# Output product of a hybrid block as four column groups of Strassen's seven products, in place of sixteen straight weight blocks

## The chip, the cores and the metric

The kernel runs on one core of a Trainium2 chip. Its time is device microseconds of one execution, median of several runs. A profiled execution of the same program gives the trace; its span and its own time stand in the table below.

## What is computed

One layer of a block with three branches (gated delta rule, S5 state space, cross attention with a memory) for 512 rows of 2048 channels in float32. The change touches only the end of it:

```
gates = sigmoid(gate_raw).reshape(b, s, 3, D)
merged = gates[:, :, 0] * p_a + gates[:, :, 1] * p_b + gates[:, :, 2] * p_c
h = h + merged @ w_out[l]          # [512 x 2048] @ [2048 x 2048]
return rmsnorm(h, final_g)
```

Every float32 product runs as three fp32r products: each operand is split in a rounded part and what the rounding left, and high x high, high x low and low x high are summed in PSUM.

## The kernel before

The program is written engine by engine, with an explicit semaphore for each hand-over; nothing reorders the instructions of an engine. TensorE is called PE below, VectorE DVE, ScalarE ACT, GpSimd POOL, SyncE SP. Constants: P = 128, S = 512, D = 2048, KW = 8 tiles of 1024, KD = 16 tiles of 2048, NT = 4 row tiles.

Weights come in blocks of 128x2048 floats, alternating between two slots. SP loads a block into `raw` in two halves, ACT copies each half to `wh` (L442, rounded), DVE writes `raw - wh` to `wl` (L450), and PE waits for that. A half is free again when PE has counted `w_used`.

Before the output product three branch products run (`products`, 8 blocks each). DVE multiplies each result by its gate from PSUM (L2261) and adds it to `merged` (L2263). In the third branch ACT and DVE also split each finished tile of `merged` into `uh` and `ul` (L1635, L2248). The moving operand is 512 columns wide.

The output product (`output`, called for four column groups `c` of 512 columns) takes 16 blocks B_OUT to B_OUT + 15. A block holds four k tiles; for each, and for each of four row tiles `m`, three matmuls of 128x512 add into bank 4 * (c % 2) + m. In all that is 4 x 16 x 4 x 3 = 768 matmuls. At a group's end DVE adds the residual `xr` from PSUM (L2297), ACT squares the sum (L1665) for the norm, DVE multiplies by the gain `fg` (L2313), and POOL only issues the next loads of `xr` (L778). In the last group the row tiles end one after another; for each, sum, root, reciprocal and scaling follow (L2302 to L2308, L1671), and SP stores two halves of the row tile.

POOL computes only in the mixer stage, from about 440 to 1490 us, where it makes tables and demodulates the S5 states (L663, L664, L666, tensor_tensor instructions of 128x512 with both inputs in SBUF) beside DVE's L450.

## Time and profile before

| | us |
|---|---|
| median of 3 runs | 2097.92 (2096.86 to 2097.95) |
| profiled execution, its own time | 2097.53 |
| its span | 2095.8 |
| PE busy | 2067.8 (99%) |
| DVE busy | 1267.3 (60%) |
| ACT busy | 804.7 (38%) |
| POOL busy | 744.7 (36%) |

The span is the profiled program from its first to its last instruction; the execution's own time is 1.7 us more. The profiled execution lies within 0.4 us of the median. PE's busy time counts a matmul from its start until its result is out, and consecutive ones overlap, so a stretch is measured by the starts of matmuls, not by their length. The starts of DVE and ACT instructions also overlap the ends of those before by about 0.1 us.

### The profile page before, as it was taken

Reading aid. Unit: us, or ns where it says so; the run is one execution under the profiler, and the core shown is the slowest. Engines: PE = TensorE matmul, PEld = TensorE weight load, DVE = VectorE, ACT = ScalarE, POOL = GpSimd, SP = SyncE. Lnnn points to the kernel's source line nnn. Section 1 sums busy time; section 2 is a strip of 40 time slices with the busy share of each in tenths; the row PEclk is TensorE's granted clock in tenths of the full one; section 3 lists DMA queues with packets and bytes.
Section 4 is the critical chain, followed back from the end, with each engine's and each line's share of the span. In section 5 each row is a group of like instructions: output and inputs, shape, how many; then the busy total and the mean of one; then the engine's idle time right before and its main releaser. Section 6 shows DMA issues by size and latency. Waiting matters only on the chain.

```text
span 2095.8 us, 30735 instructions
## 1 busy us (share of the span) xinstructions
PE 2067.8 (99%) x12124; PEld 1691.8 (81%) x12124; DVE 1267.3 (60%) x1779; ACT 804.7 (38%) x1055; POOL 744.7 (36%) x555
## 2 busy tenths in 40 slices
PE   7999999999999999999999999999999999999998
PEld 6799888888787787877878778777778888888886
DVE  6554353439688596885968959676433335454333
ACT  5433232353344533445334443453242222232223
POOL 0000000038576585765857658577201000100000
PEclk9999999999999999999999999999999999999999
DMA  8244343453343433434334343343356565553334
GB/s 258 61 127 135 102 134 91 114 135 91 104 116 94 121 97 104 115 95 120 97 104 114 96 117 100 104 117 102 103 169 207 173 184 150 180 151 110 112 123 149
DMA packets 382913, 260.63 MB, mean 124 GB/s; under 512 B 23769, under 2 KB 351810, under 8 KB 382146
## 3 DMA queue, kind: packets, MB, share of 16 engines
q1 hardware_dynamic: 364146, 203.16, 35.6%
q0 software_dynamic: 11408, 43.00, 5.9%
q10 hardware_dynamic: 7232, 12.72, 1.6%
q8 instruction: 87, 1.43, 0.3%
q14 instruction: 40, 0.33, 0.1%
HBM read 223.17 MB, written 27.28 MB: 119 GB/s over the span
## 4 chain that ended last, share of the span: by engine, by line
PE 94%; DVE 2%; DMA 1%; ACT 1%; issue 1%; POOLq 0%; ACTq 0%; DVEq 0%
PE bank L456 29%; PE bank L458 28%; PE bank L457 28%; PE bank L1097 1%; PE bank L979 1%; PE bank L991 1%; DMA yst<-s_out 1%; DVE wl L450 1%; PE bank L1046 0%; PE bank L1087 0%; PE bank L952 0%; PE bank L1035 0%; PE bank L1088 0%; PE bank L1077 0%; PE bank L1060 0%
## 5 line engine op out<-in xcount | busy, mean ns | idle before, releaser
L456 PE MATMUL bank<-uh,wh 128*128 128x512 f32 x2048 | 826.1, 403 | 2.9 <-DVE wl L450 2.7
L458 PE MATMUL bank<-uh,wl 128*128 128x512 f32 x2048 | 799.3, 390 | 0.0
L457 PE MATMUL bank<-ul,wh 128*128 128x512 f32 x2048 | 799.0, 390 | 0.0
L450 DVE TENSOR_TENSOR wl<-raw,wh 128x1024 fp32r<-128x1024 f32 x352 | 468.6, 1334 | 476.3 <-ACT wh L442 475.0
L442 ACT ACTIVATE wh<-raw 128x1024 fp32r<-128x1024 f32 x352 | 370.2, 1058 | 552.2 <-DMA raw<-in_w_in_dram 182.0
L456 PEld LDWEIGHTS bank<-uh,wh 128*128 128x128 f32 x2048 | 384.7, 188 | 90.5 <-issue 10.0
L458 PEld LDWEIGHTS bank<-uh,wl 128*128 128x128 f32 x2048 | 384.4, 188 | 83.5
L457 PEld LDWEIGHTS bank<-ul,wh 128*128 128x128 f32 x2048 | 385.2, 188 | 74.1 <-issue 1.9
L622 POOL DMA_DIRECT2D gated_c<-ox x8 | 4.3, 543 | 372.6 <-DVE ox L1808 371.9
L663 POOL TENSOR_TENSOR hr<-tcos,gr 128x512 f32<-128x512 f32 x32 | 51.7, 1615 | 199.4 <-DVE gi L2138 199.3
L1449 ACT ACTIVATE gk<-bank 128x512 f32<-128x512 f32 x48 | 28.7, 598 | 192.0 <-PE bank L458 192.0
L456 PE MATMUL bank<-gh,wh 128*128 128x512 f32 x256 | 100.9, 394 | 0.0
L458 PE MATMUL bank<-gh,wl 128*128 128x512 f32 x256 | 100.4, 392 | 0.0
L456 PE MATMUL bank<-wh,uh 128*128 128x512 f32 x256 | 99.6, 389 | 0.0
L458 PE MATMUL bank<-wh,ul 128*128 128x512 f32 x256 | 99.6, 389 | 0.0
L457 PE MATMUL bank<-wl,uh 128*128 128x512 f32 x256 | 99.6, 389 | 0.0
L457 PE MATMUL bank<-gl,wh 128*128 128x512 f32 x256 | 99.4, 388 | 0.0
L740 POOL DMA_DIRECT2D gates<-gates x24 | 17.1, 712 | 207.8 <-DVE merged L2263 136.1
L456 PE MATMUL bank<-mh,wh 128*128 128x256 f32 x256 | 73.6, 288 | 5.5 <-DVE wl L450 5.5
L458 PE MATMUL bank<-mh,wl 128*128 128x256 f32 x256 | 72.6, 283 | 0.0
L457 PE MATMUL bank<-ml,wh 128*128 128x256 f32 x256 | 72.5, 283 | 0.0
L664 POOL TENSOR_TENSOR karg<-tsin,gi 128x512 f32<-128x512 f32 x32 | 64.8, 2026 | 0.0
(355 smaller groups left out, 2826.1 us busy)
## 6 DMA issues: line engine op xcount, KB each, us to landing
raw<-in_w_in_dram SPq DMA_DIRECT2D x224, 512.0 KB, 3.9
raw<-in_w_kv_mem_dram SPq DMA_DIRECT2D x32, 512.0 KB, 4.0
raw<-in_w_out_dram SPq DMA_DIRECT2D x32, 512.0 KB, 3.6
gates<-gk ACTq DMA_DIRECT2D x48, 256.0 KB, 4.3
gates<-gates POOLq DMA_DIRECT2D x24, 512.0 KB, 4.7
raw<-in_s_w_glu_dram SPq DMA_DIRECT2D x16, 512.0 KB, 4.0
raw<-in_w_br_c_dram SPq DMA_DIRECT2D x16, 512.0 KB, 3.9
raw<-in_w_br_a_dram SPq DMA_DIRECT2D x16, 512.0 KB, 4.0
```

Source lines behind the costliest of these rows:

```text
L442: act.activation(k.wh[slot][:, c], k.raw[slot][:, c], ACT.Copy).then_inc(k.w_hi, 1)
L450: dve.tensor_tensor(k.wl[slot][:, c], k.raw[slot][:, c], k.wh[slot][:, c].bitcast(F32), ALU.subtract).then_inc(k.w_lo, 1)
L456: pe.matmul(o, ah, bh, start=start, stop=False)
L457: pe.matmul(o, ah, bl, start=False, stop=False)
L458: return pe.matmul(o, al, bh, start=False, stop=stop)
L663: pool.tensor_tensor(o[:, :], c1[:, :], a[:, :], ALU.mult).then_inc(k.dem, 1)
L664: pool.tensor_tensor(k.karg[:, :], c2[:, :], b[:, :], ALU.mult).then_inc(k.dem, 1)
L740: pool.dma_start([k.gates0, k.gates1][m % 2][:, :, :], k.gates_d[row:row + 2 * P, :] .rearrange("(t p) s -> p t s", p=P)).then_inc(k.gt_in ...
L979: mm = pe.matmul(ps[2][r:r + B, n * B:(n + 1) * B], k.lbt[r:r + B, n, :], k.tb[r:r + B, n, :], start=True, stop=True)
L991: mm = pe.matmul(ps[6][r:r + B, n * B:(n + 1) * B], k.ub[r:r + B, n, :], k.xb5[r:r + B, n, :], start=True, stop=True)
L1097: mm = pe.matmul(ps[5][r, :], k.bc[:, n, r], h[q][:, :], start=n == 0, stop=n == 1)
L1449: act.activation(k.gk[n][:, :], o[:, :], ACT.Sigmoid).then_inc(k.mx_out, 1)
```

## The change

The output product is rewritten as Strassen's scheme on halves. `merged` (transposed, channels on partitions) is cut into low and high channels (tiles i and KW + i) and into the first and last 256 rows; `w_out` into upper and lower rows and into left and right columns. Seven products of 256x1024x256 blocks replace eight. The columns are taken in four groups `g`; a group has eight units `t` (one k tile of each half), so there are 32 units `n`. A unit has seven products, each of 2 x 3 matmuls with 256 moving columns: 42 matmuls. Each product of a group has a PSUM bank of its own; the eighth bank lets the next group begin. In the last group products 2 and 3 are left to the end and summed straight in PSUM (`last_row`, 96 matmuls), so that a unit there has 30.

For each unit, SP loads four pieces of 128x256 of `w_out` to `wr` (three slots). Per unit the engines then do:

- POOL `weight_differences`: one subtraction of 128x256.
- ACT `copy_second` (128x256), `weights_x` (128x768, in the last group 128x256), `weights_y` (128x1024): the copies that round.
- DVE `weight_sums` (128x512), `weights_x` (128x768, in the last group 128x256), `weight_sums_two` (128x512), `weights_y` (128x1024). All of them have both inputs in SBUF.

Both engines, and POOL, wait with unit n + 1 until PE has finished unit n - 1 (`y_part`), since `wph` and `wpl` have two slots.

The sums of `merged` are made by POOL (`merged_sums`, four instructions of 128x256 for each of eight pairs, the last two pairs after the last merge), and are split by ACT and DVE as tiles of 128x768; the low tiles of `merged` are split only in the first units (`LATE`, `EARLY`, `SUMS` list which unit carries which: eight and two tiles of 128x512, two of 128x768). At a group's end ACT copies products 1, 2 and 3 out of PSUM, DVE combines products 6, 7, 4 and 5 with them (five instructions of 128x512, each with one input in PSUM), and POOL makes the six additions to `hrow` (`add_first`, `add_shared`) and four multiplications by the gain (`row_gains`), all of 128x2x256 with both inputs in SBUF, during the units t = 0 to 4 of the next group. `hrow` is preloaded with x. In the third branch the low and high parts of the activations now use `uh` and `ul` instead of `gh` and `gl`, and the branch tiles are taken in pairs that alternate between the low and the high half.

The core of the diff:

```diff
...
+            k.wr = sb(area, "wr", [3, 4, QC])
...
+            k.sxh = sb(area, "sxh", [3, KW, QC], F32R)
+            with ExitStack() as a:
+                k.sraw = sb(a, "sraw", [3, KW, QC])
+            k.sxl = sb(area, "sxl", [3, KW, QC], F32R)
...
+QC = 256
+GROUPS = D // (2 * QC)
+UNITS = GROUPS * KW
+ORDER = (1, 2, 3, 6, 7, 4, 5)
+FIRST = (3, 2, 6, 4, 5, 1, 7)
+SHARED = (1, 6, 7, 4, 5)
+PIECE = {1: 0, 3: 1, 2: 2, 5: 3, 7: 4, 6: 5, 4: 6}
+Y_PART = slice(3, 7)
+
...
+    def output_weights(n):
+
+        g, t = divmod(n, KW)
+        if n == 0:
+            sp.wait_ge(k.gb_st0, 8 * KW)
+            sp.wait_ge(k.gb_st1, 8 * KW)
+        if n < 3:
+            sp.wait_ge(k.w_hi, 2 * (B_OUT - 2) + n + 1)
+        wait(sp, k.w_sum, 2 * (n - 2))
+        if n > 2:
+            sp.wait_ge(k.m_sum, differences_done(n - 3))
+            sp.wait_ge(k.w_hi, rounded(n - 3, 0))
+        wait(sp, k.w_lo, x_part(n - 3) if n > 2 else 0)
+        for half in range(2):
+            row = (t + KW * half) * P
+            sp.dma_start(k.wr[:, n % 3, 2 * half:2 * half + 2, :],
+                         k.w_out[row:row + P, :].rearrange("p (h c) -> p h c", h=2)[:, :, g * QC:(g + 1) * QC]).then_inc(k.w_in_half[n % 3], 16)
+
+    def input_columns(g):
+
...
+    def last_weights(v):
+
+        n = UNITS + v
+        sp.wait_ge(k.w_sum, 2 * min(n - 2, UNITS))
+        sp.wait_ge(k.m_sum, differences_done(min(n - 3, UNITS - 1)))
+        sp.wait_ge(k.w_lo, x_part(n - 3) if n - 3 < UNITS else last_part(n - 3 - UNITS))
+        for t in (2 * v, 2 * v + 1):
+            row = (KW + t) * P
+            sp.dma_start(k.wr[:, n % 3, 2 * (t % 2):2 * (t % 2) + 2, :],
+                         k.w_out[row:row + P, :].rearrange("p (h c) -> p h c", h=2)[:, :, (GROUPS - 1) * QC:GROUPS * QC]).then_inc(k.w_in_half[n % 3], 16)
+
...
+    def merged_sums(i):
+
+        lo, hi, s = k.merged[:, i, :], k.merged[:, KW + i, :], k.sraw
+        n = sums_done(i) - 4
+        if i == 0:
+            pool.wait_ge(k.g_lo, 3 * KW)
+        tt = pool.tensor_tensor
+        tt(s[:, 0, i, :], lo[:, QC:S], hi[:, QC:S], ALU.add).then_inc(k.m_sum, 1)
+        pool.wait_ge(k.m_sum, n + 1)
+        tt(s[:, 1, i, :], s[:, 0, i, :], lo[:, 0:QC], ALU.subtract).then_inc(k.m_sum, 1)
+        tt(lo[:, QC:S], lo[:, 0:QC], lo[:, QC:S], ALU.subtract).then_inc(k.m_sum, 1)
+        pool.wait_ge(k.m_sum, n + 2)
+        tt(s[:, 2, i, :], hi[:, 0:QC], s[:, 1, i, :], ALU.subtract).then_inc(k.m_sum, 1)
...
+    def weight_differences(n):
+
+        w = k.wr[:, n % 3, :, :]
+        pool.wait_ge(k.w_in_half[n % 3], 8 * B_OUT + 32 * (n // 3 + 1))
+        if n < 2:
+            pool.wait_ge(k.w_used, 2 * (B_OUT - 1 + n))
+        else:
+            pool.wait_ge(k.w_used, y_part(n - 2))
+        pool.tensor_tensor(k.wyr[n % 2][:, 6, :], w[:, 2, :], w[:, 3, :], ALU.subtract).then_inc(k.m_sum, 1)
...
+    def row_gains(g, m):
+        pool.wait_ge(k.h_sq, 4 * g + TAIL_ROWS.index(m) + 1)
+        o = output_columns(k, [m], g)
+        pool.tensor_tensor(o, o, k.fg[:, :, :], ALU.mult).then_inc(k.h_fg, 1)
+
+    def add_first(g):
+
+        pool.wait_ge(k.xr_in, 64 * (g + 1))
+        for half, n, v in ((1, 1, k.gk0), (1, 2, k.c2), (0, 3, k.c3)):
+            if g == GROUPS - 1 and n > 1:
+                continue
+            pool.wait_ge(k.o_p1, 3 * g + n)
+            if n == 2:
+                pool.wait_ge(k.o_add, 6 * g + 1)
+            o = quarter(k, 0, half, g)
+            pool.tensor_tensor(o, o, halves(v[:, 0:S]), ALU.add).then_inc(k.o_add, 1)
+
+    def add_shared(g, part):
+
+        rows, half, v = ((1, 1, k.t3), (1, 0, k.t3), (0, 0, k.gk1))[part]
+        pool.wait_ge(k.o_ev, 5 * g + 3 + part)
+        if part == 2 and g < GROUPS - 1:
+            pool.wait_ge(k.o_add, 6 * g + 3)
+        o = quarter(k, rows, half, g)
+        pool.tensor_tensor(o, o, halves(v[:, 0:S]), ALU.add).then_inc(k.o_add, 1)
 
...
+    for n in range(3, UNITS):
+        g, t = divmod(n, KW)
+        if n + 1 < UNITS:
+            weight_differences(n + 1)
+        if t == 0 and g:
+            add_first(g - 1)
+        if t == 1 and g:
+            add_shared(g - 1, 0)
+            add_shared(g - 1, 1)
+        if t == 2 and g:
+            add_shared(g - 1, 2)
+            pool.wait_ge(k.fg_in, 16 * g)
+        if t in (3, 4) and g:
+            for m in (2, 3) if t == 3 else (0, 1):
+                row_gains(g - 1, m)
+        if t == 5 and g:
+            pool.wait_ge(k.h_fg, 4 * g)
+            load_gains(g)
+    add_first(GROUPS - 1)
+    for part in range(3):
+        add_shared(GROUPS - 1, part)
 
...
+    def product(n, p, last_x, last_y):
+
+        g, t = divmod(n, KW)
+        r = ORDER.index(p)
+        bank = ps[(7 * g + r) % 8]
+        if p in (1, 2, 3):
+            pe.wait_ge(k.w_lo, x_part(n))
+        else:
+            pe.wait_ge(k.w_lo, y_part(n))
+        if g == 0:
+            pe.wait_ge(k.m_lo, operand_count("low" if p in (1, 7) else "high" if p in (2, 4) else "sums", t))
+        if n == 0:
+            wait(pe, k.mrg, {4: 2 * KD - 2, 5: 2 * KD - 1}.get(p, 2 * KD - 3 if p == 7 else 0))
+        elif t == 0 and r == 0:
+            if g == 1:
+                pe.wait_ge(k.mrg, 2 * KD)
+            wait(pe, k.o_ev, 5 * (g - 1))
+        elif t == 0 and r < 4:
+            pe.wait_ge(k.o_p1, 3 * (g - 1) + r)
+        elif t == 0:
+            pe.wait_ge(k.o_ev, 5 * (g - 1) + r - 3)
+        order = product_order(n)
+        after_x = t == KW - 1 and p == order[order.index(last_x) + 1]
+        after_unit = t == 0 and r == 0 and g
+        hi, lo = operand(p, t)
+        wh, wl = k.wph[n % 2][:, PIECE[p], :], k.wpl[n % 2][:, PIECE[p], :]
+        for i in range(2):
+            a, o = slice(i * P, (i + 1) * P), bank[:, i * QC:(i + 1) * QC]
+            mm = pe.matmul(o, hi[:, a], wh, start=t == 0 and i == 0, stop=False)
+            if i == 0 and (after_x or after_unit):
+                mm.then_inc(k.w_used, 1)
+            pe.matmul(o, hi[:, a], wl, start=False, stop=False)
+            mm = pe.matmul(o, lo[:, a], wh, start=False, stop=t == KW - 1 and i == 1)
+        if t == KW - 1:
+            mm.then_inc(k.o_ps, 1)
+        elif p in (last_x, last_y):
+            mm.then_inc(k.w_used, 1)
+
+    for n in range(UNITS):
+        order = product_order(n)
+        last_x = [p for p in order if p in (1, 2, 3)][-1]
+        last_y = [p for p in order if p > 3][-1]
+        for p in order:
+            product(n, p, last_x, last_y)
+
+    def last_row(i, t):
...
+    def copied_product(g, p):
+        order = product_order(KW * g + KW - 1)
+        act.wait_ge(k.o_ps, 7 * g + order.index(p) + 1)
+        wait(act, k.o_add, 6 * g)
+        act.activation([k.gk0, k.c2, k.c3][p - 1][:, 0:S], ps[(7 * g + ORDER.index(p)) % 8][:, :], ACT.Copy).then_inc(k.o_p1, 1)
...
+    late, early, sums = LATE, EARLY, SUMS
+    for n in range(UNITS):
+        g, t = divmod(n, KW)
+        if n < len(late):
+            late_hi(late[n][0])
+        if n < len(late) and len(late[n]) > 1:
+            late_hi(late[n][1])
+        if n + 1 < UNITS:
+            copy_second(n + 1)
+            weights_x(n + 1)
+        if n == UNITS - 1:
+            last_hi(0)
+        if t == KW - 1:
+            copied_product(g, 1)
+            if g < GROUPS - 1:
+                copied_product(g, 2)
+                copied_product(g, 3)
+        if n + 1 < UNITS:
+            weights_y(n + 1)
+        if n in early:
+            early_hi(early[n])
+        if n in sums:
+            sums_hi(sums[n])
+        if t in (2, 3) and g:
+            for m in (2, 3) if t == 2 else (0, 1):
+                row_squares(g - 1, m)
+
...
+    def weight_sums(n):
+
+        w, y = k.wr[:, n % 3, :, :], k.wyr[n % 2]
+        dve.wait_ge(k.w_in_half[n % 3], 8 * B_OUT + 32 * (n // 3 + 1))
+        if n < 2:
+            dve.wait_ge(k.w_used, 2 * (B_OUT - 1 + n))
+        else:
+            dve.wait_ge(k.w_used, y_part(n - 2))
+        tt(y[:, 3:5, :], w[:, 1:3, :], w[:, 0:1, :].to_broadcast([P, 2, QC]), ALU.subtract).then_inc(k.w_sum, 1)
+
+    def weight_sums_two(n):
+
+        y = k.wyr[n % 2]
+        dve.wait_ge(k.w_sum, 2 * n + 1)
+        dve.wait_ge(k.m_sum, differences_done(n))
+        dve.wait_ge(k.w_hi, rounded(n, 0))
+        tt(y[:, 5:7, :], y[:, 5:7, :], y[:, 3:4, :].to_broadcast([P, 2, QC]), ALU.add).then_inc(k.w_sum, 1)
+
+    def weights_x(n):
+        dve.wait_ge(k.w_hi, rounded(n, 1))
+        m = 3 if n < UNITS - KW else 1
+        tt(k.wpl[n % 2][:, 0:m, :], k.wr[:, n % 3, 1:1 + m, :], k.wph[n % 2][:, 0:m, :].bitcast(F32), ALU.subtract).then_inc(k.w_lo, 1)
+
+    def last_lo(v):
+        dve.wait_ge(k.w_hi, last_rounded(v))
+        a = slice(4 * (v % 2), 4 * (v % 2) + 4)
+        tt(k.wpl[v // 2][:, a, :], k.wr[:, (UNITS + v) % 3, :, :], k.wph[v // 2][:, a, :].bitcast(F32), ALU.subtract).then_inc(k.w_lo, 1)
+
...
+    def fourth(g):
+        bank = finish(g, 4)
+        dve.wait_ge(k.xr_in, 64 * (g + 1))
+        o = quarter(k, 1, 1, g)
+        tt(o, o, halves(bank), ALU.subtract).then_inc(k.o_ev, 1)
+
+    def fifth(g):
+        bank = finish(g, 5)
+        o = quarter(k, 1, 0, g)
+        tt(o, o, halves(bank), ALU.subtract).then_inc(k.o_ev, 1)
+        tt(k.gk1[:, :], k.gk1[:, :], bank, ALU.subtract).then_inc(k.o_ev, 1)
...
+    late, early, sums = LATE, EARLY, SUMS
+    for n in range(UNITS):
+        g, t = divmod(n, KW)
+        last = n == UNITS - 1
+        if n < len(late):
+            late_lo(late[n][0])
+        if n < len(late) and len(late[n]) > 1:
+            late_lo(late[n][1])
+        if not last:
+            weight_sums(n + 1)
+            weights_x(n + 1)
+            weight_sums_two(n + 1)
+        if t == KW - 1 and not last:
+            sixth(g)
+            seventh(g)
+        if not last:
+            weights_y(n + 1)
+        if n in early:
+            early_lo(early[n])
+        if n in sums:
+            sums_lo(sums[n])
+        if t == KW - 1 and not last:
+            fourth(g)
+        if t == 0 and g:
+            fifth(g - 1)
+
+    g = GROUPS - 1
+    last_lo(0)
```

The order on DVE at the end of the first column group. Before, two rows stand for the two halves of each weight block; `bank0` to `bank3` are the group's four row tiles:

```order
L450 TENSOR_TENSOR wl0<-raw0,wh0 128x1024 x2
L450 TENSOR_TENSOR wl1<-raw1,wh1 128x1024 x2
L450 TENSOR_TENSOR wl0<-raw0,wh0 128x1024 x2
L2297 TENSOR_TENSOR hrow<-bank0,xr 128x512
L2297 TENSOR_TENSOR hrow<-bank1,xr 128x512
L2297 TENSOR_TENSOR hrow<-bank2,xr 128x512
```

After, on DVE, from unit 8's weights at the end of group 0 into group 1 (`raw0` and `raw1` now hold the sums, `cst` and `gk1` intermediate results):

```order
L2607 TENSOR_TENSOR raw0<-wr 128x512
L2620 TENSOR_TENSOR wl0<-wr,wh0 128x768
L2615 TENSOR_TENSOR raw0<-raw0 128x512
L2641 TENSOR_TENSOR gk1<-gk0,bank3 128x512
L2646 TENSOR_TENSOR cst<-gk1,bank4 128x512
L2629 TENSOR_TENSOR wl0<-raw0,wh0 128x1024
L2652 TENSOR_TENSOR hrow<-hrow,bank5 128x2x256
L2607 TENSOR_TENSOR raw1<-wr 128x512
L2620 TENSOR_TENSOR wl1<-wr,wh1 128x768
```

Where one kind of instruction fed PE, four do now, the last of which (L2629) needs ACT's rounding of what the third (L2615) wrote.

The order on POOL in the output product. Before, it only issues loads:

```order
L740 DMA gates1<-gates 128x2x512
L740 DMA gates0<-gates 128x2x512
L740 DMA gates1<-gates 128x2x512
L778 DMA xr<-in_x_dram 128x512 x12
L116 UNCONDITIONAL_BRANCH
```

After, on POOL, units 8 to 12 (the first units of group 1):

```order
L908 TENSOR_TENSOR raw1<-wr 128x256
L929 TENSOR_TENSOR hrow<-hrow,gk0 128x2x256
L929 TENSOR_TENSOR hrow<-hrow,c2 128x2x256
L929 TENSOR_TENSOR hrow<-hrow,c3 128x2x256
L908 TENSOR_TENSOR raw0<-wr 128x256
L938 TENSOR_TENSOR hrow<-hrow,cst 128x2x256 x2
L908 TENSOR_TENSOR raw1<-wr 128x256
L938 TENSOR_TENSOR hrow<-hrow,gk1 128x2x256
L908 TENSOR_TENSOR raw0<-wr 128x256
L917 TENSOR_TENSOR hrow<-hrow,fg 128x2x256 x2
L908 TENSOR_TENSOR raw1<-wr 128x256
L917 TENSOR_TENSOR hrow<-hrow,fg 128x2x256 x2
```

POOL has computing work in the whole output product now, one L908 a unit and ten larger instructions a group.

## Rows read from the trace of the kernel before

**Rows 1.** Page, part 1: busy us (share of the span) xinstructions of an engine.

```profile
PE 2067.8 (99%) x12124; PEld 1691.8 (81%) x12124; DVE 1267.3 (60%) x1779; ACT 804.7 (38%) x1055; POOL 744.7 (36%) x555
```

**Rows 2.** Timeline (start us, us, engine, instruction), PE: the output's first and last matmuls.

```profile
1913.54 0.39 PE L458 MATMUL bank<-gh,wl 128*128 128x512 f32 x1
1913.76 0.40 PE L456 MATMUL bank<-wh,uh 128*128 128x512 f32 x1
...
2087.67 0.39 PE L458 MATMUL bank<-wh,ul 128*128 128x512 f32 x1
```

**Rows 3.** Timeline, PE: first and last of 85 matmuls in a row with 256 columns.

```profile
120.05 0.28 PE L456 MATMUL bank<-mh,wh 128*128 128x256 f32 x1
...
129.94 0.28 PE L456 MATMUL bank<-mh,wh 128*128 128x256 f32 x1
```

**Rows 4.** Timeline, DVE and ACT: a half of a weight block being split in the output.

```profile
1983.18 1.06 ACT L442 ACTIVATE wh<-raw 128x1024 fp32r<-128x1024 f32 x1 [4.40 <-DMA raw<-in_w_out_dram]
...
1984.27 1.23 DVE L450 TENSOR_TENSOR wl<-raw,wh 128x1024 fp32r<-128x1024 f32 x1 [4.23 <-ACT wh L442]
```

**Rows 5.** Timeline, DVE: starts of instructions that follow one another without a wait.

```profile
602.53 1.23 DVE L450 TENSOR_TENSOR wl<-raw,wh 128x1024 fp32r<-128x1024 f32 x1
603.67 0.68 DVE L2131 TENSOR_TENSOR ma<-bank,tcos 128x512 f32<-128x512 f32 x1
604.27 0.68 DVE L2132 TENSOR_TENSOR mb<-bank,tsin 128x512 f32<-128x512 f32 x1
604.99 0.69 DVE L2134 TENSOR_TENSOR gr<-ma,mb 128x512 f32<-128x512 f32 x1
```

**Rows 6.** Timeline, POOL and DVE in the mixer stage: where both compute from SBUF.

```profile
638.62 1.29 POOL L663 TENSOR_TENSOR hr<-tcos,gr 128x512 f32<-128x512 f32 x1 [7.30 <-DVE gi L2138]
639.87 2.28 POOL L664 TENSOR_TENSOR karg<-tsin,gi 128x512 f32<-128x512 f32 x1
...
638.98 2.01 DVE L450 TENSOR_TENSOR wl<-raw,wh 128x1024 fp32r<-128x1024 f32 x1
640.92 1.52 DVE L1981 TENSOR_SCALAR kc<-kraw,cwh 128x512 f32<-128x512 f32 x1
```

**Rows 7.** Timeline, POOL and DVE a little later: a reader of PSUM beside POOL.

```profile
645.25 2.28 POOL L664 TENSOR_TENSOR karg<-tcos,gi 128x512 f32<-128x512 f32 x1
...
646.90 0.65 DVE L2131 TENSOR_TENSOR ma<-bank,tcos 128x512 f32<-128x512 f32 x1
```

**Rows 8.** Busy time by stretch (start:end us, length, busy us xcount, granted clock, DMA share, GB/s).

```profile
30.00:32.00 2.00, 1.95 (x17) 1.00 1.16 340
32.00:34.00 2.00, 0.00 (x0) 1.00 0.43 131
34.00:36.00 2.00, 1.92 (x9) 0.55 0.93 262
36.00:38.00 2.00, 2.00 (x13) 0.60 1.01 253
38.00:40.00 2.00, 2.00 (x19) 1.00 0.08 13
```

**Rows 9.** Timeline, ACT and DVE: the last row tile's way to its store.

```profile
2088.15 0.68 DVE L2297 TENSOR_TENSOR hrow<-bank,xr 128x512 f32<-128x512 f32 x1
...
2090.34 0.49 DVE L2307 TENSOR_SCALAR hrow<-hrow,stat 128x512 f32<-128x512 f32 x1
2090.74 0.75 DVE L2308 SCALAR_TENSOR_TENSOR hrow<-hrow,stat,fg 128x512 f32<-128x512 f32 x1
```

394 lines of the change are left out of this document (260 added, 134 removed).

## Prediction

> **What bounds the kernel now.** The page's first part comes first: PE is busy for 99% of the span, DVE for 60%, POOL for 36% [rows 1]. So the time is what PE's stream takes, and in the output product I read it by starts of matmuls: 768 of them, the first at 1913.76, the last at 2087.67 [rows 2], which is 173.91 / 767 = 0.2267 us apart. No wait lies between them, since the branch's last matmul starts 0.22 before. From the first of them to the span's end are 2095.8 - 1913.76 = 182.0 us, 8.1 of them behind the last start. That is the part that the change rewrites. Its weights come by ACT, then DVE, then PE [rows 4], and DVE idles over 4 us before each half block, ample cover for what PE needs.
>
> **What PE gains.** The matmuls become 256 columns wide. The nearest rows are 85 of the same width and number format in a row in the attention stage [rows 3]: 9.89 / 84 = 0.1177 us apart, at full clock. A unit of 42 then takes 4.94 us, one of the last group (30) 3.53, and the 96 of the last rows 11.3. The sum is 24 x 4.94 + 8 x 3.53 + 11.3 = 158.1 us against 173.9: **15.8 us less**, if nothing else ends later. The waits that now stand before each product are the only thing those rows lack; I take nothing for them, since 0.1177 holds across the block boundaries there.
>
> **What each unit asks of DVE and ACT.** PE is fed by a chain that I price from starts. A DVE instruction of 1024 columns occupies 1.14 us (602.53 to 603.67) and one of 512 columns 0.60 [rows 5]; 768 and 256 columns I put between and below, at 0.87 and 0.33. If the next needs the result, 0.72 passes for 512 (604.27 to 604.99) [rows 5]. ACT's 1024 take 1.06, and DVE starts 0.03 later [rows 4]. A unit's chain on DVE is weight_sums 0.60, weights_x 0.87, weight_sums_two 0.72 until ACT may start, ACT's weights_y 1.09, DVE's weights_y 1.14: **4.4 us**, and 3.9 in the last group. DVE stands in order, so during ACT's 1.09 it does nothing, and the next unit's chain begins only behind it. Against PE's 4.94 this alone is hidden with 0.5 to spare; against 3.53 it isn't, which costs 8 x 0.4 = 3 us in the last group. In group 0 DVE also has ten tiles of 512 and two of 768 to split, 7.7 us, against a reserve of 8 x 0.5: 4 to 6 us more. The combination at a group's end (five instructions, 3 us) fits in the reserve and, in part, in ACT's 1.09. Loads are no term: they have three slots, so two units' time.
>
> **What POOL takes from DVE.** Before, POOL computes nothing beside the output product. Now it has, for each of the groups 1 to 3, ten instructions of 512 elements and eight of 256. What that does is visible in the mixer stage [rows 6]. DVE's L450 starts at 638.98, while POOL's L663 runs until 639.91, and takes 2.01 us instead of 1.23: it was held for 0.78, that is until 0.15 before POOL's end. POOL's next instruction starts at 639.87 and takes 2.28 instead of 1.29, as if it began when L450 ended at 640.99; DVE's next takes 1.52 and ends 0.3 behind POOL's. They take turns, one instruction each, and neither overlaps the other. A DVE instruction that reads PSUM is not held: 0.65 beside a POOL instruction [rows 7]. All four of DVE's weight instructions have two inputs in SBUF, like L450; so have all of POOL's new ones.
>
> The Trainium skill states this as a rule (SBUF — State Buffer, Who interferes with whom): a DVE instruction with two SBUF inputs and a GpSimd instruction that reads SBUF exclude one another for the whole instruction. The trace agrees, with the 0.78 and 2.28 above; by this rule the change would lose more than it gains, and the sum by it is the one that follows.
>
> The price of a POOL instruction, when DVE has work queued, is its 1.27 less 0.15, so 1.1 us for 512 elements. For 256 there is no row; half of 1.27 is the lower bound, the whole the upper one, and I take 0.7, so 0.55 held. A unit in which POOL has two large instructions and the weight difference then takes 4.4 + 2 x 1.1 + 0.55 = **7.2 us** on DVE's chain, against PE's 4.94. What is spared is only POOL's work that falls in the 1.2 us in which DVE waits for ACT.
>
> - Groups 1 and 2, each: of the units t = 0 to 4 four meet two or three large ones (t = 0 three additions, one of which I let fall in DVE's wait), 4 x 7.2; one of them also has two combinations, 1.2; four units at 4.94. Together 49.8; the two weight slots absorb about 1. So 48.8 against 39.5: **9.3 more each**. If every POOL instruction used DVE's waits first (8 x 1.2 of 15.4 held) it would be 44.2: 5 more. If none did, 54: 14 more.
> - Group 3: 4 x (3.9 + 2.2 + 0.55) + 1.2 + 4 x 4.1 = 44.2 against 28.2: **16 more** (12 to 21).
> - Group 0: 8 x 4.4 + 7.7 + 0.6, and POOL's eight sums of merged and eight weight differences, of which some 6 us hold DVE: 49.4 against 39.5: **9.9 more** (5 to 14).
> - Last rows: their weights are split while DVE combines products 6, 7, 4 and 5 in turn, and the fourth pair's load waits until the first has been split: one wait of about **1.4 us**.
> - Tail: before, 8.1 us from the last start to the end, of which the last row tile takes 2088.15 to 2090.34 for sum, square, root, then the scaling [rows 9] and the store. After, scaling has one product more of 768 columns in place of 512, and the tiles before it queue on DVE and ACT, since their additions end late: **1.8 more** (0 to 3).
>
> **Sum.** 2097.53 (the profiled execution; 0.4 under the median, which I neglect) - 15.8 + 9.9 + 2 x 9.3 + 16 + 1.4 + 1.8 = 2129.4. I predict **2129 us**, 1.5% slower. With the lower bounds of the groups (5 + 10 + 12) it is 2112, with the upper ones (14 + 28 + 21) 2148. What else moves: in the third branch ACT's first tile waits for half a block more of PE, but the weight copy behind it could start no earlier; POOL's sums there run where DVE idles 3 us between merges. Both cost nothing; without that cover they would cost below 2 us.
>
> **The rivals.**
>
> *POOL doesn't hold DVE, and only the chain counts.* Speaks for it: DVE idles a lot, and POOL's instructions could slip into its waits. Against it: those waits are 1.2 us a unit, POOL's work in five units of a group 3.3 a unit. Price: group 0 +5.5, group 3 +5, last rows and tail +3: 2097.5 - 15.8 + 13.5 = 2095, within 0.2% of before. Between this and my case lie partial sharing and shorter POOL instructions, up to 2112.
>
> *The other side: PE's gain comes through.* If neither POOL nor the chain reaches past PE's stream (ACT and DVE overlapping better than in my chain, so that group 3 keeps to 3.53), there remain the last rows and the tail: 2097.5 - 15.8 + 3 = 2085, faster. It decides where a unit's chain stays below 4.94 with POOL beside it, and below 3.53 in the last group; 3.3 of DVE's own time plus ACT's 1.09 speak against the first as soon as POOL takes 0.6, and 2.8 plus 1.09 against the second.
>
> *The clock falls.* PE would stand still 2.3 us in each loaded unit, 3 in the last group. In the attention stage, after 2.1 us without a matmul, the granted clock is 0.55 and 0.60 for two stretches of 2 us, the lower level of 1.2 GHz for most of them, and back at 1.00 after [rows 8]. Half a unit at the lower level costs 2 to 2.5 us, about what PE would have stood still, so I take nothing for it. If it lasts through loaded units, these twelve (and four in group 0) cost 1 to 2 more: 2145 to 2160.
>
> The Trainium skill's page TensorE: Matmul & The Clock Gate (HAM oscillation) warns of just such gaps between bursts of matmuls; rows 8 agree, and by it the last rival gains weight over a plain sum.
>
> **How the numbers follow.** I give my case with its bounds (2112 to 2148) 0.58, the stretch between 2102 and 2112 0.08, no hold (2094 to 2102) 0.10, PE's gain coming through (below 2094) 0.12, the clock (above 2148) 0.12. A measurement of this kernel can tell some 0.2%, 4.2 us, from no change. So slower: 0.78, the same: 0.10, faster: 0.12. The range takes in my bounds, the gap and the no-hold case, and the lower part of the clock's: 2096 to 2150, with about 0.8.
>
> **What would show it.** By stretches, PE's busy time in the output product would be well below full, about 70% in the units t = 0 to 4 of groups 1 and 2 and lower in group 3, with idle time that ends with DVE's wl. Matmul starts would be 0.118 apart inside a product. DVE's instructions of 512 and 768 columns would last 1.1 us longer beside POOL's additions and gains, and POOL's longer than 1.27. Group starts, seen at the first matmul of units 8, 16 and 24, would lie some 49 us apart, the last group's end 44 behind. I am wrong if those groups last 40 us (no hold), if POOL's small instruction takes much less or more than 0.7, or if matmuls start further apart than 0.118 without a wait, either by the clock or by the semaphore waits.

## The result, and the profile after

The changed kernel takes 2128.1 us (median of 4 runs, 2126.8 to 2128.7), the kernel before 2097.6 in the same session: ratio 1.0148, 95% interval 1.0136 to 1.0160. The prediction was 2129. The profiled execution has a span of 2125.1 us; before it was 2095.8.

Page of the changed kernel, part 1 (busy us, share of the span, instructions), against [rows 1]: PE is 5 us less busy in a span that is 29 us longer, and DVE and POOL are each busy for over 110 us more.

```profile
PE 2062.9 (97%) x12700; PEld 1712.1 (81%) x12700; DVE 1381.5 (65%) x1881; ACT 849.8 (40%) x1142; POOL 863.8 (41%) x640
```

Timeline of PE, changed kernel: the first matmul of each column group, the first of the last rows, and the last one of all. It answers to [rows 2].

```profile
1912.51 0.28 PE L1479 MATMUL bank<-wh,sxh 128*128 128x256 f32 x1
...
1962.52 0.28 PE L1479 MATMUL bank<-wh,uh 128*128 128x256 f32 x1
...
2010.06 0.28 PE L1479 MATMUL bank<-wh,uh 128*128 128x256 f32 x1
...
2059.07 0.28 PE L1479 MATMUL bank<-wh,uh 128*128 128x256 f32 x1
...
2103.16 0.28 PE L1508 MATMUL bank<-wh,sxh 128*128 128x256 f32 x1
...
2114.88 0.28 PE L1512 MATMUL bank<-wh,ul 128*128 128x256 f32 x1
```

The differences between the starts are the lengths of the four groups: **50.0, 47.5, 49.0 and 44.1 us**, then 11.7 for the last rows and 10.2 for the tail (from the last start to the end of the span). Without a wait a group of 336 matmuls takes 40.0 us (the second run below) and the last one, of 240, about 29. What PE waits for, 1905 to 2126 us (waiting engine and line, releaser: us in total, times, longest):

```profile
PE bank L1479 <- DVE wl L2629: 25.7, 20, 3.4
PE bank L1479 <- DVE wl L2620: 2.8, 4, 1.0
PE bank L1479 <- DVE sxl L2597: 2.1, 1, 2.1
```

Nearly all of it is for DVE's last instruction of a unit's chain. Why DVE is late stands in its timeline and in POOL's, here in the first two units of group 1 (start us, duration us, engine, instruction, idle before and what ended it):

```profile
1964.31 2.04 DVE L2620 TENSOR_TENSOR wl<-wr,wh 128x768 fp32r<-128x768 f32 x1
1966.27 1.77 DVE L2615 TENSOR_TENSOR raw<-raw 128x512 f32<-128x512 f32 x1
...
1970.91 0.67 DVE L2657 TENSOR_TENSOR hrow<-hrow,bank 128x512 f32<-128x512 f32 x1
...
1972.10 1.83 DVE L2607 TENSOR_TENSOR raw<-wr 128x512 f32<-128x512 f32 x1
...
1978.23 0.68 DVE L2607 TENSOR_TENSOR raw<-wr 128x512 f32<-128x512 f32 x1
1978.83 0.95 DVE L2620 TENSOR_TENSOR wl<-wr,wh 128x768 fp32r<-128x768 f32 x1
1979.70 0.69 DVE L2615 TENSOR_TENSOR raw<-raw 128x512 f32<-128x512 f32 x1
```

```profile
1963.75 1.78 POOL L929 TENSOR_TENSOR hrow<-hrow,gk 128x512 f32<-128x512 f32 x1
1965.68 3.52 POOL L929 TENSOR_TENSOR hrow<-hrow,c 128x512 f32<-128x512 f32 x2
1969.15 0.75 POOL L908 TENSOR_TENSOR raw<-wr 128x256 f32<-128x256 f32 x1
1969.86 3.52 POOL L938 TENSOR_TENSOR hrow<-hrow,cst 128x512 f32<-128x512 f32 x2
```

From 1963.75 to 1973.4 POOL works through, and three of DVE's instructions last 1.09, 1.08 and 1.15 us longer than the same three from 1978.23 on, where POOL is idle. L2657, which reads PSUM (bank), keeps its 0.67 in the middle of it.

By stretches (start:end us, length, busy us xcount of PE, PEld, DVE, ACT, POOL, then the granted clock): units t = 0 to 4 of group 1, the rest of it, nearly the same units of group 2, and the first 28 us of group 3, most of its units t = 0 to 4.

```profile
1962.50:1993.60 31.10, 26.18 (x212) 25.16 (x210) 26.50 (x23) 12.23 (x22) 23.44 (x16) 1.00 0.47 149
1993.60:2010.00 16.40, 15.29 (x126) 15.09 (x127) 12.92 (x15) 8.94 (x13) 4.65 (x4) 1.00 0.36 113
2010.00:2042.00 32.00, 27.41 (x212) 26.65 (x211) 27.41 (x23) 12.41 (x23) 23.08 (x15) 0.95 0.26 83
2059.00:2087.00 28.00, 19.74 (x136) 18.52 (x136) 23.50 (x22) 10.08 (x22) 20.76 (x15) 0.91 0.29 94
```

### The profile page after: what moved, and what is told of

Its sections match the earlier page's. It is cut to its first block, busy times and chain, and to the rows that moved or that the text cites. A ratio compares the mean times of both kernels' runs of the same rounds, so it can differ in the third digit from the quotient of the medians.

```text
span 2125.1 us, 32408 instructions
## 1 busy us (share of the span) xinstructions
PE 2062.9 (97%) x12700; PEld 1712.1 (81%) x12700; DVE 1381.5 (65%) x1881; ACT 849.8 (40%) x1142; POOL 863.8 (41%) x640
## 4 chain that ended last, share of the span: by engine, by line
PE 86%; DVE 7%; ACT 3%; issue 2%; DMA 2%; POOL 1%; POOLq 0%; ACTq 0%; DVEq 0%
PE bank L526 26%; PE bank L528 25%; PE bank L527 25%; DVE wl L2620 1%; DVE raw L2615 1%; DVE raw L2607 1%; PE bank L1479 1%; ACT wh L1918 1%; PE bank L1483 1%; PE bank L1482 1%; PE bank L1304 1%; DVE wl L520 1%; PE bank L1186 1%; PE bank L1198 1%; DVE wl L2629 1%
## 5 line engine op out<-in xcount | busy, mean ns | idle before, releaser
L526 PE MATMUL bank<-uh,wh 128*128 128x512 f32 x2176 | 875.8, 402 | 2.3 <-DVE wl L520 2.1
L528 PE MATMUL bank<-uh,wl 128*128 128x512 f32 x2176 | 849.1, 390 | 0.0
L527 PE MATMUL bank<-ul,wh 128*128 128x512 f32 x2176 | 848.8, 390 | 0.0
L520 DVE TENSOR_TENSOR wl<-raw,wh 128x1024 fp32r<-128x1024 f32 x320 | 430.3, 1347 | 383.0 <-ACT wh L512 381.6
L526 PEld LDWEIGHTS bank<-uh,wh 128*128 128x128 f32 x2176 | 408.7, 188 | 95.0 <-issue 10.4
L1699 ACT ACTIVATE gk<-bank 128x512 f32<-128x512 f32 x48 | 28.7, 598 | 188.6 <-PE bank L528 188.6
L1479 PE MATMUL bank<-wh,sxh 128*128 128x256 f32 x176 | 52.6, 299 | 28.9 <-DVE wl L2629 25.7
L908 POOL TENSOR_TENSOR raw<-wr 128x256 f32<-128x256 f32 x32 | 35.7, 1116 | 88.1 <-PE bank L1483 66.5
L1479 PE MATMUL bank<-wh,uh 128*128 128x256 f32 x240 | 69.7, 290 | 1.8 <-DVE wl L2620 1.8
L772 POOL TENSOR_SCALAR karg<-cst,s5h 128x512 f32<-128x512 f32 x32 | 24.5, 765 | 112.2 <-DVE hph L2270 96.9
L1482 PE MATMUL bank<-wl,uh 128*128 128x256 f32 x240 | 69.3, 289 | 0.0
L1483 PE MATMUL bank<-wh,ul 128*128 128x256 f32 x240 | 69.1, 288 | 0.0
```

The lines of the kernel that those rows point to most:

```text
L520: dve.tensor_tensor(k.wl[slot][:, c], k.raw[slot][:, c], k.wh[slot][:, c].bitcast(F32), ALU.subtract).then_inc(k.w_lo, 1)
L526: pe.matmul(o, ah, bh, start=start, stop=False)
L527: pe.matmul(o, ah, bl, start=False, stop=False)
L528: return pe.matmul(o, al, bh, start=False, stop=stop)
L908: pool.tensor_tensor(k.wyr[n % 2][:, 6, :], w[:, 2, :], w[:, 3, :], ALU.subtract).then_inc(k.m_sum, 1)
L1479: mm = pe.matmul(o, hi[:, a], wh, start=t == 0 and i == 0, stop=False)
```

## The experiments

**Theory A** is the prediction's: while a POOL instruction reads the SBUF, a DVE instruction with two inputs there is held, 1.1 us for each large one, and so a loaded unit's chain overruns PE. **Theory B**: the chain DVE, ACT, DVE is too long by itself. **C**: PE loses the time itself, by its clock or its semaphores. **D**: POOL, with its large instructions ahead, makes the difference that DVE needs too late. Most kernels differ from the changed one in one thing; those that combine several stand last. The lengths of groups come from the profiled execution of each kernel, the times are medians. The kernel before took 2097.6 us beside the changed one and 2096.5 to 2096.9 beside the kernels below, so a difference of about 1 us between one of them and the 2128.1 is not told apart from none.

### POOL's large instructions on one column

```diff
-        o = output_columns(k, [m], g)
-        pool.tensor_tensor(o, o, k.fg[:, :, :], ALU.mult).then_inc(k.h_fg, 1)
+        o = output_columns(k, [m], g)[:, :, 0:1]
+        pool.tensor_tensor(o, o, k.fg[:, :, 0:1], ALU.mult).then_inc(k.h_fg, 1)
```

(and so in `add_first` and `add_shared` for g < 3; the other columns' sums and gains are left out)

> The changed kernel (2128.1 us, column groups of 50.0, 47.5, 49.0 and 44.1 us), with one thing taken away: the ten sums and gains of 512 columns a row that POOL makes for each of the first three groups, during the units of the next group, touch one column a half only. Their order and all semaphores stay; left out of the computation are the sums and gains of the other columns. Theory A (DVE is held while POOL works on the SBUF, and a loaded unit is 2 to 3.5 us longer for it): the loaded units fall from 6.4 to 8.9 us to the 5.0 of units without these sums; groups 1 and 2 come to 40 us each (7.5 and 9 less), group 3 to 33 to 36 (8 to 11 less), group 0 stays at 50; 2100 to 2104 us in all. DVE's instructions of 512 and 768 columns in groups 1 to 3 stand at 0.7 and 0.95 us but where the small difference of 256 columns still runs beside them. Theory B (the chain from DVE over ACT back to DVE is simply too long for a unit, POOL or not): groups 1 and 2 stay at 47 to 49, and the time stays within 2 us of 2128. Theory C (TensorE's clock): it would stay too, since nothing of PE is changed.

Measured: 2102.8 us, 25 less and inside A's range; groups 51.5, 40.1, 41.1 and 35.3. Groups 1 and 2, by stretches (columns as above):

```profile
1963.60:2003.70 40.10, 40.10 (x338) 40.01 (x337) 31.94 (x37) 21.45 (x35) 15.99 (x19) 1.00 0.50 161
2003.70:2044.80 41.10, 40.74 (x339) 40.26 (x338) 32.94 (x39) 21.37 (x36) 16.43 (x19) 1.00 0.35 111
```

PE is at work throughout group 1 and for all but 0.4 us of group 2. The chain, with nothing else changed, fits in PE's 5.0 us a unit, so B by itself is out for groups 1 and 2, and so is C. Group 1 is the clean measure, with a granted clock of 1.00 in both kernels: 7.4 us less. Group 0 has gained nothing, as A said. One unit of it took 6.6 us instead of 5.1, and that is the clock: PE stood idle for 2.10 us before 1952.03, and the granted clock was 0.50 and 0.65 in the two stretches of 2 us from 1952 on. In the changed kernel it stood idle for 2.09 us before the same unit, and the clock stayed at 1.00.

### The same, and no POOL instruction in a unit

```diff
-        tt(y[:, 5:7, :], y[:, 5:7, :], y[:, 3:4, :].to_broadcast([P, 2, QC]), ALU.add).then_inc(k.w_sum, 1)
+        tt(y[:, 5, :], w[:, 2, :], y[:, 3, :], ALU.add).then_inc(k.w_sum, 1)
+        dve.wait_ge(k.w_sum, 3 * n + 2)
+        tt(y[:, 6, :], y[:, 5, :], w[:, 3, :], ALU.subtract).then_inc(k.w_sum, 1)
```

(POOL's `weight_differences` and ACT's `copy_second` fall away)

> The kernel of the run before (large sums and gains on one column a half, the rest of them left out), and in addition POOL has no instruction of its own in a unit: the difference of 256 columns is not made by POOL and the copy of 256 columns not by ACT, but DVE makes the two blocks that hang on them, each with one instruction of 256 columns, in place of the one of 512; the same weight sums come out. DVE's chain in a unit is then 0.7, 0.95, twice 0.4, ACT's 1.06 and DVE's 1.23 us, 4.7 to 4.8 us with nothing held, and one wait more on DVE's own result. Theory A (hold): every unit of groups 0 to 2 is bound by PE at 4.94 or by this chain at up to 5.1; group 0, where the differences and merged operands' work alone cost 10.5 us before, falls from 50 to 40 to 44; in all 2088 to 2096 us. Theory B (chain alone): DVE's own work in a unit has not become less, so group 0 stays at 50 and the time is that of the run before within 2 us.

Measured: 2100.8 us; groups 49.9, 40.0, 40.0 and 34.1. That is 2 us under the run before, at the edge of B and outside A's 2088 to 2096: A was wrong on group 0. The weight differences hold DVE there too, but their absence gives nothing back in sum: the two instructions of 256 columns (0.43 us each) take 0.2 us a unit more of DVE than the one of 512, and what makes group 0 long is for the most part something else. One thing still holds DVE there, POOL's `merged_sums`: six entries of DVE's timeline from 1918.21 to 1926.4 (seven instructions) last 3.5 us longer in all than the same ones undisturbed, for instance L2601 1.23 for 0.68.

### POOL writes only

```diff
-        pool.tensor_tensor(o, o, halves(v[:, 0:S]), ALU.add).then_inc(k.o_add, 1)
+        for _ in range(2):
+            pool.memset(o, 1.0).then_inc(k.rows_zero, 1)
+            zn[0] += 1
+            pool.wait_ge(k.rows_zero, zn[0])
+        pool.memset(o, 1.0).then_inc(k.o_add, 1)
```

(in a helper, for all ten; their results are left out)

> The changed kernel, with each of POOL's ten large sums and gains a group (groups 0 to 2) replaced by three fills of the same 512 columns, one after the other, which write but read nothing; order and semaphores stay, and the results of these sums are left out of the computation. POOL is then busy for a time of the same order at the same places. Theory A in its narrow form (POOL and DVE shut each other out only while POOL also reads the SBUF): as with the sums on one column, 2100 to 2106 us. Theory A in its wide form (any POOL work on the SBUF holds DVE): groups 1 and 2 stay at 46 to 49 us, 2120 to 2129 us. Theory D (not the hold costs the time, but POOL itself, which comes late to the difference of 256 columns of the next unit because its large sums are ahead of it): stays at 2118 to 2128 as far as the fills take as long as the sums, with DVE's instruction L2615 waiting for POOL and DVE's durations undisturbed (0.7 and 0.95 us).

Measured: 2104.2 us, inside the range of A's narrow form. POOL and DVE at the start of group 1:

```profile
1962.85 1.11 POOL L923 MEMSET hrow<- 128x512 f32 x2
1964.02 0.53 POOL L926 MEMSET hrow<- 128x512 f32 x1
1964.66 1.11 POOL L923 MEMSET hrow<- 128x512 f32 x2
1965.83 0.53 POOL L926 MEMSET hrow<- 128x512 f32 x1
1966.30 1.11 POOL L923 MEMSET hrow<- 128x512 f32 x2
1967.46 0.53 POOL L926 MEMSET hrow<- 128x512 f32 x1
1967.95 0.75 POOL L908 TENSOR_TENSOR raw<-wr 128x256 f32<-128x256 f32 x1
```

```profile
1963.41 0.95 DVE L2635 TENSOR_TENSOR wl<-wr,wh 128x768 fp32r<-128x768 f32 x1
1964.28 0.69 DVE L2630 TENSOR_TENSOR raw<-raw 128x512 f32<-128x512 f32 x1
```

POOL comes to its difference (L908) 5.1 us after it began the fills; in the changed kernel it was 5.4 (1963.75 to 1969.15). So it is equally late, and nothing is lost; and in the changed kernel DVE never stands idle before L2615, which needs that difference: D is out. DVE's 0.95 and 0.69 beside the fills are undisturbed. What holds DVE is POOL's instructions that read the SBUF, not that POOL works or writes.

### The large instructions on DVE

```diff
...
+        if g:
+            slot(g - 1, t)
         if not last:
             weights_y(n + 1)
```

(`slot` makes in units 0, 1, 2, 4 and 5 two of the sums and gains each; POOL's for groups 0 to 2 fall away)

> The changed kernel with full computation; POOL's ten large sums and gains of groups 0 to 2 are made by DVE, right before its instruction of 1024 columns, where it waits 1.1 us for ACT in each unit: two sums in each of units 0, 1 and 2 of the next group, two gains in units 4 and 5. The last group's remain on POOL. Each should take DVE 0.6 to 0.7 us, so a pair 1.3 less the 1.1 of waiting. Theory A (hold): the loaded units were 2 to 3.5 us over 5.0; they come to 5.0 to 5.6; groups 1 and 2 to 41 to 43 us, group 3 to 36 to 39; 2105 to 2112 us in all. Theory B (chain alone): DVE gets 6.5 us more work a group and nothing is freed, so groups 1 and 2 are 1 to 3 us longer than now, 2130 to 2136 us.

Measured: 2106.4 us, inside A's range; groups 50.0, 40.4, 41.8 and 37.6. DVE makes ten more instructions a group and the kernel is 22 us faster: 0.69 us of DVE's own cost less than the 1.1 us for which POOL's hold it, and part of them lies in the wait for ACT. Of the single changes with full computation this one gives the most.

### POOL starts where DVE waits

```diff
+        if t < 5 and g:
+            pool.wait_ge(k.w_sum, 2 * (n + 1) + 2)
         if t == 0 and g:
             add_first(g - 1)
```

> The changed kernel with one more wait and full computation: before its large sums and gains in units 0 to 4 of a group, POOL waits until DVE has made the second weight sum of the next unit, so that the first of them starts where DVE has nothing to do but wait 1.13 us for ACT. Theory A (hold): of the two or three holds of 1.1 us in a loaded unit one falls into that wait; 13 loaded units (the 15 less those with room) give back 0.5 to 1.1 us each, 2114 to 2121 us in all. Theory D (POOL comes late with the difference of 256 columns): POOL is later by the time it waits, so the loaded units become 1 to 2 us longer, 2135 to 2150 us. It is an open question which part wins when a pair of sums of 1.8 us each no longer ends before the next unit's first DVE instruction; a result within 2 us of 2128 would say that the hold is only moved.

Measured: 2119.2 us, inside A's range. D's loss appears only once in group 1 and once in group 2: DVE stands idle for 0.70 and 0.69 us before L2617, until POOL's difference is made. The second instruction of each pair still meets DVE's next one, at its full price: L2609 takes 1.78 us at 1988.24, for 0.69.

### ACT and DVE in halves

```diff
-        act.activation(k.wph[n % 2][:, Y_PART, :], k.wyr[n % 2][:, Y_PART, :], ACT.Copy).then_inc(k.w_hi, 1)
+        for a in (slice(3, 5), slice(5, 7)):
+            act.activation(k.wph[n % 2][:, a, :], k.wyr[n % 2][:, a, :], ACT.Copy).then_inc(k.w_hi, 1)
```

(and so in DVE's `weights_y`)

> The changed kernel with full computation; ACT rounds the four weight blocks of the second kind as two instructions of 512 columns instead of one of 1024 (1.06 us), and DVE makes their low parts as two of 512, the first while ACT is at the second. DVE's wait for ACT falls from 1.13 to about 0.6 us a unit, DVE's own work rises by 0.1. Theory B (the chain from DVE over ACT back to DVE is a bound of its own where DVE is late): each of the 20 units in which PE waits for L2629 is about 0.4 to 0.5 us shorter, 2118 to 2121 us. If the hold alone mattered (DVE free otherwise), the same instructions are held as before and the time stays within 2 us of 2128. PE-bound units stay at 5.0.

Measured: 2121.7 us, 6.4 less, just above B's range and not A's "no change". DVE's wait for ACT fell from 1.13 to 0.70 a unit. Part of the 6.4 can be the clock: PE ran through one stretch at the lower level here and through three in the changed kernel, at about 1.4 us each (see the rivals below). In groups 0 and 1, where the clock fell in neither, 1.5 and 1.1 us are gained. So where the hold has made DVE late, the chain is worth its full length as well: A and B aren't alternatives, their terms add.

### The merged operands' low parts in DVE's wait

```diff
...
+        if n == 0:
+            late_lo(0)
         if not last:
             weight_sums(n + 1)
             weights_x(n + 1)
             weight_sums_two(n + 1)
+        if n < len(late):
+            for i in late[n][n == 0:]:
+                late_lo(i)
...
```

(`early_lo` and `sums_lo` follow there too; the calls that stood elsewhere fall away)

> The changed kernel with full computation and only an order changed: the low parts of the merged operands that DVE makes during group 0 (eight of the kind late, two early, two sums, 0.7 to 0.95 us each) stand behind the second weight sum, where DVE waits 1.13 us for ACT, instead of ahead of the unit's weight sums or behind its last instruction (the first, which unit 0 needs at once, stays; ACT's instruction for the early and sums kinds goes ahead of its own wait likewise). Groups 1 to 3 are untouched. Theory B (group 0's 10.5 us over PE's time are the chain plus this work on DVE, not the hold: with large sums and differences off POOL it still took 49.9): of the 11 moved 0.6 to 1.1 us are hidden in each of seven units, group 0 falls from 50.0 to 43 to 46, and the time to 2121 to 2124 us. Theory A (the hold by POOL's merged sums and differences makes group 0 long): less than 2 us change.

Measured: 2122.4 us, inside B's range, group 0 at 45.75 instead of 50.0, groups 1 and 2 as before (47.6, 48.8). So over 4 of group 0's 10.5 us are this work on DVE. The rest is one unit of 10.4 us. There DVE's instructions, such as L2620 with 1.49 for 0.95, run beside eight POOL instructions in `merged_sums`: a hold again, in the one place where POOL's small instructions stand in a row. Two things add to it in this run. DVE stands idle for 1.40 us before L2615 at 1922.82, because POOL makes the difference for it only behind the first four of those sums: that is D's mechanism. And after PE's idle time of 3.79 us the granted clock was 0.50 from 1928 to 1930.

### The sums on DVE, POOL's large ones kept

The edit of the second run, on the changed kernel.

> The changed kernel with full computation; only POOL's difference of 256 columns and ACT's copy of 256 in every unit are gone, and DVE makes the two blocks that hang on them in two instructions of 256 columns (0.43 us each) in place of one of 512 (0.69 us). POOL's large sums stay. Theory A (hold): the difference holds DVE by 0.4 to 0.5 us a unit (L2607 in undisturbed units took 1.1 to 1.2 instead of 0.69), which is gained in the units where DVE is late (about 20), and 0.2 us of own work is paid: 2119 to 2125 us; the large sums, no longer behind a difference, may also fall on other DVE instructions. Rival (a hold costs as long as POOL is busy, whoever is ahead): the same number. Theory B: DVE's own chain is 0.2 us longer in 20 units, 2130 to 2133 us.

Measured: 2128.1 us, no change, and neither theory's number (2119 to 2125, 2130 to 2133). The means of DVE's instructions say why. Groups of DVE's instructions in the output (busy us, mean ns, idle before), first the changed kernel, then this run:

```profile
L2629 DVE TENSOR_TENSOR wl<-raw,wh 128x1024 fp32r<-128x1024 f32 x31 | 42.9, 1385 | 31.5 <-ACT wh L1918 31.5
L2620 DVE TENSOR_TENSOR wl<-wr,wh 128x768 fp32r<-128x768 f32 (+1 forms) x31 | 35.2, 1134 | 0.7 <-ACT wh L1912 0.5
L2607 DVE TENSOR_TENSOR raw<-wr 128x512 f32<-128x512 f32 x31 | 34.4, 1111 | 0.2 <-PE bank L1483 0.2
L2615 DVE TENSOR_TENSOR raw<-raw 128x512 f32<-128x512 f32 x31 | 28.7, 926 | 0.0
```

```profile
L2611 DVE TENSOR_TENSOR wl<-wr,wh 128x768 fp32r<-128x768 f32 (+1 forms) x31 | 39.9, 1288 | 0.0
L2620 DVE TENSOR_TENSOR wl<-raw,wh 128x1024 fp32r<-128x1024 f32 x31 | 38.3, 1236 | 31.5 <-ACT wh L1910 31.5
L2597 DVE TENSOR_TENSOR raw<-wr 128x512 f32<-128x512 f32 x31 | 30.1, 970 | 1.6 <-PE bank L1475 1.6
L2604 DVE TENSOR_TENSOR raw<-wr,raw 128x256 f32<-128x256 f32 x31 | 16.7, 539 | 0.0
L2606 DVE TENSOR_TENSOR raw<-raw,wr 128x256 f32<-128x256 f32 x31 | 16.5, 533 | 1.1
```

The instructions of 1024 and the first of 512 columns lost 4.6 and 4.3 us of hold, the 768 gained 4.7 (POOL's large ones now meet it), and the second sums are 4.5 longer: 28.7 before, 33.2 now. It adds to about zero.

### One large POOL instruction a unit, in DVE's wait

```diff
+        if n + 1 < UNITS:
+            pool.wait_ge(k.w_sum, 3 * (n + 1) + 3)
+        if t < 3:
+            add_first(g - 1, t)
+        elif t < 6:
+            add_shared(g - 1, t - 3)
```

(with the edits of the two runs before; the gains in pairs in t = 6 and 7)

> Full computation; POOL keeps its ten large sums and gains, but one a unit (the gains in pairs in units 6 and 7), each started when DVE has made the second weight sum of the next unit and begins to wait 1.13 us for ACT; its differences are made by DVE as in the run with the sums on DVE, and group 0's late operands stand in that wait. Theory A in the form 'a hold costs only what DVE would have done in that time': a POOL sum of 1.3 us beside a wait of 1.13 us costs 0.2 us, units of 4.7 us on DVE stay under PE's 5.0, groups 1 and 2 come to 40 to 42 us though POOL does the same work as in the changed kernel; group 3 (DVE's chain 4.1 us a unit) to 35 to 39; 2098 to 2106 us. If POOL's sums cost their hold wherever they stand, groups 1 and 2 stay at 46 to 48, over 2115 us.

Measured: 2101.0 us, inside A's range; groups 45.3, 40.0, 41.5 and 35.9. DVE, then POOL, at the end of a unit of group 1:

```profile
1970.98 0.41 DVE L2605 TENSOR_TENSOR raw<-wr,raw 128x256 f32<-128x256 f32 x1
1971.42 0.42 DVE L2607 TENSOR_TENSOR raw<-raw,wr 128x256 f32<-128x256 f32 x1
1972.97 1.33 DVE L2621 TENSOR_TENSOR wl<-raw,wh 128x1024 fp32r<-128x1024 f32 x1 [1.12 <-ACT wh L1911]
```

```profile
1971.93 1.29 POOL L927 TENSOR_TENSOR hrow<-hrow,c 128x512 f32<-128x512 f32 x1 [3.43 <-DVE raw L2607]
```

POOL does the same ten large instructions a group as in the changed kernel. The six sums take 1.29 us each instead of 1.7 to 1.8, and DVE's L2621 is held for 0.10 (1.33 for 1.23) instead of 1.1. The four gains still run in pairs, at a mean of 1.88 us, in units with room for it: group 1 takes 40.0 all the same. What a hold costs is a matter of place, not of the amount of POOL's work.

### All of it, and the low part of the first weights in the wait

```diff
...
             weight_sums(n + 1)
-            weights_x(n + 1)
             weight_sums_two(n + 1)
+            weights_x(n + 1)
...
```

(with: large instructions on DVE, second sums on DVE, halves, merged operands' low parts in the wait)

> A version with full computation that puts together what the runs so far point to: POOL keeps only the merged operands' sums of group 0 and the last group's sums; its large sums and gains and its differences are made by DVE (two instructions of 256 columns for the latter), ACT's rounding and DVE's low parts of the second kind of weights in two halves, group 0's late operands where DVE waits for ACT, and DVE's low part of the first kind of weights (0.95 us) there too, behind the weight sums. DVE's work in a unit is then 0.7 + 0.45 + 0.45 + 0.95 + 1.35 = 3.9 us without a wait, and the chain over ACT 0.7 + 0.9 + 0.6 + 1.35 = 3.5. Theory A and B together (hold, and a chain that is too long): groups 1 and 2 at 40 to 41.5 us, group 3 at 35 to 38, group 0 at 43 to 46 (POOL's merged sums hold DVE there still), in all 2096 to 2101 us. If a part of the loss were PE's own (semaphores, clock), it would stay over 2103.

Measured: **2096.0 us** (2094.9 to 2097.8) against 2096.9 for the kernel before in that session: ratio 0.9997, interval 0.9987 to 1.0007, at the lower end of what was expected. The five stretches of the output:

```profile
1912.00:1956.00 44.00, 40.75 (x337) 40.11 (x336) 42.21 (x63) 24.76 (x40) 9.64 (x9) 1.00 0.46 142
1956.00:1996.40 40.40, 40.39 (x339) 40.17 (x339) 37.83 (x64) 19.58 (x35) 0.72 (x1) 1.00 0.52 165
1996.40:2036.70 40.30, 40.29 (x338) 40.06 (x337) 37.20 (x64) 18.72 (x35) 0.73 (x1) 1.00 0.36 115
2036.70:2070.90 34.20, 30.25 (x243) 28.97 (x242) 32.04 (x60) 15.09 (x31) 2.37 (x2) 1.00 0.38 121
2070.90:2084.30 13.40, 12.04 (x98) 11.47 (x96) 10.23 (x16) 7.90 (x14) 3.96 (x4) 1.00 0.29 103
```

32 us are recovered, and the scheme breaks even. DVE is busy for 42.2 of 44.0 and 32.0 of 34.2 us in groups 0 and 3: there it is the bound now. PE saves 1/8 of the work in its matmuls, and DVE pays for it, at 163 us in the whole output for 64 before.

### The same with group 0's work spread

```diff
-LATE = ((0, 1), (2, 3), (4,), (5,), (6, 7))
-EARLY = {2: 6, 3: 7}
-SUMS = {5: 6, 6: 7}
+LATE = ((0, 1), (2,), (3,), (4,), (5,), (6,), (7,))
+EARLY = {1: 6, 2: 7}
+SUMS = {4: 6, 5: 7}
```

(and POOL waits for w_sum 12 ahead of `merged_sums(7)`; the first residual load stands one unit later)

> The first kernel of this call with group 0's work on the merged operands spread further: one low operand a unit instead of two in units 1 and 4, and POOL's second set of merged sums two units later than its first, with the load of the residual one unit later. Same total of DVE work; the hold by POOL's eight instructions of 256 columns falls on two units instead of one. With 1.0 us of slack on DVE in each unit, group 0 should fall by 1 to 3 us against that kernel: 2094 to 2099 us, about the time of the kernel before. If the hold is simply added wherever it falls, no change against that kernel.

Measured: 2097.8 us, inside the 2094 to 2099, but the 1 to 3 us that group 0 was to give back didn't come. It is at 44.1, for 44.0 in the run before: its loss is spread over three units and its sum stays. Group 1 is 2.2 longer, with one wait of 1.8 us for a weight load that now stands behind the residual's.

## Why the prediction was right, point by point

Each term, as the profiled executions have it, against the sum of the prediction:

| term | predicted | measured |
|---|---|---|
| start of the output | 0 | -1.3 |
| group 0 over 39.5 | +9.9 | +10.5 |
| group 1 over 39.5 | +9.3 | +8.0 |
| group 2 over 39.5 | +9.3 | +9.5 |
| group 3 over 28.2 | +16 | +15.9 |
| last rows | +1.4 | +0.4 |
| tail (10.2 against 8.1) | +1.8 | +2.1 |
| sum with PE's -15.8 | +31.9 | +29.3 |

**What PE gains: right, but put a little too large.** Matmuls start 0.118 apart, but a unit without a wait takes 5.00, not 4.94, so a group of 40.0 has 0.5 us of small gaps in it that the attention stage [rows 3] lacks. That part of the groups' terms is neither hold nor chain. "I take nothing for them" was off by 1.5 to 2 us in all.

**The hold: right, in sign, size and mechanism.** Predicted 1.1 us per large instruction, measured 1.08 to 1.15; predicted 0.55 for the small one, and L2607 at 1982.65 shows 1.24 for 0.68, so 0.56. The reader of PSUM isn't held, as in [rows 7]. The first run shows the cause (7.4 us of group 1, 25 in all), the third its narrow form, the one with one large instruction a unit that the place counts. The rule of the Trainium skill that the prediction cites (SBUF — State Buffer, Who interferes with whom: a DVE instruction with two SBUF inputs and a GpSimd one that reads SBUF exclude each other) agrees with each of these, the fills included, as they don't read.

**The loaded units: nearly right in sum, wrong in shape.** I put four units a group at 7.2 us, among t = 0 to 4. In group 1 the long ones are t = 1, 2, 4 and 5, with 7.34, 6.44, 7.33 and 6.43, and the other four take 5.0. The unit t = 0 isn't late: PE works there on weights made a unit earlier. PE's share in t = 0 to 4 was to be about 70%; by starts it is 212 x 0.119 / 31.1 = 81%, since only three of these five are long.

**Group 0: right number, partly for the wrong reason.** I gave some 6 us to POOL's merged sums and weight differences and 4 to 6 to DVE's extra tiles. The tiles are worth 4.3 (moved into the wait). The differences are worth 0.1 net: 49.9 without them, DVE's dearer pair of instructions included. The merged sums' hold is 3.5 by the lengths of DVE's instructions in the second run, and group 0 is 4.0 over 40.0 in the run with everything, where only they are left on POOL. They were not taken away by themselves. With PE's small gaps (0.5) that makes 8.4 of 10.5; the last 2 us stay open.

**Group 3: right, its parts less so.** Of its 15.9 over 28.2 the large instructions are 8.8 (44.1 to 35.3), which is what 4 x 2.2 gave; but up to 2.6 of that is the clock, which I had left out, so their hold may be smaller. The other 7.1 are mostly the chain, at 4.1 to 4.4 us a unit against PE's 3.6. Without the differences 5.9 remain (34.1 over 28.2, 0.4 of it PE's small gaps), where I had put 3 for the chain and 1.2 for the combinations, and 3 for the differences' hold, which is worth 1.2 net.

**Last rows and tail.** One wait of 0.2 us for the last weights, not 1.4. In eight of the eleven kernels tried it is there, with 1.3 to 2.4 us; in the first, in the one with fills and in the one with the large instructions on DVE it is at most 0.2. What decides it was not settled. The tail was sized right.

**The start**, 1912.51 for 1913.76, lies outside the change as I priced it. 1.0 us of it is PE's one wait in the branch stages, before their first weights at 1547: 0.2 us instead of 1.2. The chain ahead of it has one load of yst with 11.17 us instead of 12.16, at 1528. All variants start at 1911.5 to 1912.5, so no cost of the third branch shows. Why that load is shorter wasn't tried.

**The rivals.** "No hold, only the chain" gave 2095. Its condition is nearly met in the second run, without the large instructions and the differences: 2100.8. Only the merged sums still hold DVE there, for 3.5 us. Taken off, that would leave some 2097 (an estimate), so the rival was about 2 us too low, and faster than before was not in reach by taking the hold away.

The clock was a smaller loss, but I had taken nothing for it. In group 2 PE stood idle for 2.09 us before 2019.46, and soon after it was granted half its speed, as in [rows 8] (the granted clock is the third number from the end: 0.84 and 0.50, mostly the lower level of 1.2 GHz):

```profile
2019.00:2021.00 2.00, 1.54 (x10) 1.54 (x11) 2.00 (x4) 0.00 (x0) 2.00 (x2) 0.84 0.35 119
2021.00:2023.00 2.00, 2.00 (x12) 2.00 (x11) 2.00 (x2) 0.00 (x0) 0.79 (x1) 0.50 0.00 0
2023.00:2025.00 2.00, 2.00 (x16) 2.00 (x16) 0.87 (x3) 1.16 (x2) 0.78 (x2) 0.81 0.00 0
```

Group 2, with the same work as group 1, is 1.5 us longer for it. Group 3 had it twice, after idle times of 3.41 and 1.97 us. In each case 14 or 15 matmuls start 0.21 us apart instead of 0.12, about 1.4 us (an estimate); I had put such a stretch at 2 to 2.5. After the idle times of 1.1 to 1.4 us in group 1 the granted clock stayed at 1.00. But the length of the idle time alone doesn't decide it: it stayed at 1.00 after 2.09 us in group 0 of the same kernel, and after 3.32 us (before 2061.56) in the run with ACT and DVE in halves.

**The sum.** The mechanism is shown, but that the sum came within 1 us of the measured time is luck: small gaps and the clock, for which I had taken nothing, cost 3.5 to 6 us, and the start, the last rows and a smaller loss in group 1 than I had put gave about as much back.

## What to carry to other kernels

Before work is given to POOL because "it is idle", look at what DVE does in that time: each POOL instruction that reads the SBUF beside a DVE instruction with two SBUF inputs costs DVE its whole length less 0.15 us, here 1.1 us, while the same work made by DVE itself costs 0.6 to 0.7. If it must be POOL, let it start where DVE waits, one instruction for a wait of its length, or let it write only. And when a scheme saves matmuls (here 1/8), price a unit's chain over the other engines against the new, shorter unit of PE: here DVE's load in the output went from 64 to 163 us, and with everything in the best place that was found the scheme breaks even.

## What the runs showed of the hardware that was not expected

- POOL's fills of 512 columns take 0.53 us each, and 90 of them beside DVE cost next to nothing: 2104.2 us against 2102.8 with one-column instructions.
- POOL's gains on 128 x 2 elements still have a mean of 0.53 us in the first run; the shortest such instruction took 0.2 (near 1958.55 in the second run).
- Taking away a hold can leave the time as it is, to about 1 us, because POOL's next instruction meets DVE's next one (the run with the sums on DVE).
- DVE's 1024 columns in two halves of 512 occupy 0.60 us each, and 1.14 in one: the split costs under 0.1 us and shortens the wait for ACT by 0.43.
- The clock doesn't fall after each idle time of a length: after 2.09 us the granted clock was 0.50 soon after in one place of the changed kernel and 1.00 in another, and 1.00 after 3.32 us in the run with halves. Where it falls in units that DVE bounds, the loss can vanish: group 0 of the second run had one such stretch, that of the run with the sums on DVE none, and both took 49.9 us.
